# One transformer block (HGRN2, convolution, SwiGLU): the low part of the channel mixer's operand moves from GpSimd to VectorE

## What is computed

```python
x = x + mx[2] * rms_norm(mix_x, post_mix_g[l])
hx = swiglu(modulate(x, pre_ffn_g[l], mx[3], mx[4]), ffn_w_gate[l], ffn_w_up[l], ffn_w_down[l])
x = x + mx[5] * rms_norm(hx, post_ffn_g[l])
# swiglu(h, wg, wu, wd) = (silu(h @ wg) * (h @ wu)) @ wd,  modulate(x, g, shift, scale) = rms_norm(x, g) * (1 + scale) + shift
```

## Time and profile before

| what | value |
|---|---|
| median of 3 runs | 1452.11 us (1450.2 to 1452.63) |
| the profiled execution | 1452.88 us, span 1451.1 us, mean granted PE clock 0.97 |
| PE busy | 1375.9 us (95%) |
| DVE busy | 778.6 us (54%) |
| ACT busy | 377.3 us (26%) |
| GpSimd busy | 324.2 us (22%) |
| `mix(0)` on PE starts | 662.50 us |
| the first `gate_up` starts | 704.28 us |
| the first `gate_up` of the third position starts | 734.13 us |

### The profile page before, as it was taken

One profiled execution on the slowest core, in us unless ns is written; L12 is line 12 of the kernel. 1 busy time (PEld: TensorE's weight loads), 2 busy tenths in 40 slices (PEclk: granted clock), 3 DMA queues, 4 the chain that ended last, 5 costly groups with the idle time before them and its releaser, 6 DMA issues. The chain is left out here.

```text
span 1451.1 us, 17647 instructions
## 1 busy us (share of the span) xinstructions
PE 1375.9 (95%) x6725; PEld 1148.5 (79%) x6725; DVE 778.6 (54%) x1020; ACT 377.3 (26%) x562; POOL 324.2 (22%) x135
## 2 busy tenths in 40 slices
PE   6699899999999997898989999999999999999998
PEld 1588788888888886687768888888888888888876
DVE  2899969769778879818721313232232313232227
ACT  3521222132232234616631121111111121111112
POOL 1522111021111124503524122122122122122110
PEclk9699799999999998999999999999999999999999
DMA  9384110110010010004321111101101111101132
GB/s 370 155 284 165 29 30 16 30 44 28 29 43 29 14 68 34 1 25 164 136 68 29 50 39 58 58 31 57 57 29 58 49 39 57 58 30 57 51 124 116
DMA packets 94704, 101.94 MB, mean 70 GB/s; under 512 B 3118, under 2 KB 77091, under 8 KB 94658
## 3 DMA queue, kind: packets, MB, share of 16 engines
q1 hardware_dynamic: 94658, 101.32, 20.5%
HBM read 92.92 MB, written 8.39 MB: 70 GB/s over the span
## 5 line engine op out<-in xcount | busy, mean ns | idle before, releaser
L1238 POOL TENSOR_TENSOR slot<-slotraw,slot 128x1024 fp32r<-128x1024 f32 x66 | 160.5, 2442 | 522.2 <-ACT slot L1174 313.8
L561 PE MATMUL bank<-h2Ta,slot 128*128 128x512 f32 x1056 | 247.5, 394 | 5.2 <-POOL slot L1238 4.9
L561 PE MATMUL bank<-slot,mid 128*128 128x512 f32 x1056 | 242.9, 391 | 1.8 <-POOL slot L1238 1.8
L561 PEld LDWEIGHTS bank<-h2Ta,slot 128*128 128x128 f32 x1056 | 200.4, 190 | 47.8 <-POOL slot L1238 5.3
L561 PEld LDWEIGHTS bank<-slot,mid 128*128 128x128 f32 x1056 | 199.3, 189 | 43.8 <-POOL slot L1238 2.2
L561 PE MATMUL bank<-cathi,slot 128*128 128x512 f32 x704 | 220.2, 389 | 0.0
L1419 DVE SCALAR_TENSOR_TENSOR cat<-conv_u,taps,cat 128x784 f32 (+29 forms) x120 | 150.6, 1255 | 12.6 <-DVE cat L1419 6.2
L561 PEld LDWEIGHTS bank<-cathi,slot 128*128 128x128 f32 x704 | 132.1, 188 | 27.7 <-issue 0.3
L561 PE MATMUL bank<-hT,ringb 128*128 128x512 f32 (+1 forms) x672 | 149.1, 378 | 0.4 <-DVE cat L1402 0.4
L1694 DVE TENSOR_TENSOR mid<-bank,sgm 128x512 f32<-128x512 f32 x44 | 30.4, 692 | 221.7 <-ACT sgm L1189 221.7
L1719 DVE TENSOR_TENSOR arena<-bank,arena 128x512 f32<-128x512 f32 x144 | 99.5, 691 | 90.0 <-PE bank L561 89.5
(11 more groups left out here) (171 smaller groups left out, 1516.7 us busy)
## 6 DMA issues: line engine op xcount, KB each, us to landing
mraw<-in_w_mod SPq DMA_DIRECT2D x48, 512.0 KB, 7.0
slotraw<-in_ffn_w_gate SPq DMA_DIRECT2D x22, 512.0 KB, 3.7
slotraw<-in_ffn_w_up SPq DMA_DIRECT2D x22, 512.0 KB, 3.8
slotraw<-in_ffn_w_down SPq DMA_DIRECT2D x22, 512.0 KB, 3.9
ringinb<-in_w_in SPq DMA_DIRECT2D x12, 512.0 KB, 3.6
xst<-in_x SPq DMA_DIRECT2D x8, 512.0 KB, 13.7
ringina<-in_w_in SPq DMA_DIRECT2D x8, 512.0 KB, 4.7
ringinc<-in_w_in SPq DMA_DIRECT2D x8, 512.0 KB, 4.7
```

The costliest lines, as they stand in the source:

```text
L561: return pe.matmul(o, l, r, start=start, stop=stop, skip_group_check=True)
L1238: return pool.tensor_tensor(lo, full, hi.bitcast(F32), ALU.subtract)
```

## The change

DVE makes the low part of h2: in step t it does so for block t - 1, behind `x2(t)`, and it waits for ACT's copy (`h2_hi`) there. GpSimd keeps the splits of the four weight slots and nothing else in this stage.

```diff
--- before.py
+++ after.py
@@ -1278,11 +1278,8 @@
                 pool.wait_ge(f_hi, no + 1)
                 lo_part(slot[i][:, 1], slot_raw[i][:, 1], slot[i][:, 0]).then_inc(f_lo, 1)
 
-            for t in range(XT):
-                pool.wait_ge(h2_hi, t + 1)
-                lo_part(h2_block(t, 1), h2f[:], h2_block(t, 0)).then_inc(h2_lo, 1)
-                if t in (0, 1, 3, 5):
-                    ffn_lo((t + 1) // 2, (t + 1) // 2)
+            for j in range(4):
+                ffn_lo(j, j)
 
             def pool_round(n, par):
                 if not first(n):
@@ -1671,6 +1668,11 @@
                                             gain2[:, k:k + 1], mod[:, 3, k, 0:1], ALU.mult, ALU.add)
                 ins.then_inc(h2_free, 1)
 
+            def h2_low(t):
+
+                dve.wait_ge(h2_hi, t + 1)
+                dve.tensor_tensor(h2_block(t, 1), h2f[:], h2_block(t, 0).bitcast(F32), ALU.subtract).then_inc(h2_lo, 1)
+
             mix_add(0)
             for t in range(XT + 1):
                 if t < XT:
@@ -1681,6 +1683,8 @@
                     h2(t - 1)
                 if t < XT:
                     x2(t)
+                if t >= 1:
+                    h2_low(t - 1)
 
             def dve_pair(n, pair, par):
 
```

## The result

The changed kernel takes **1461.15 us** (median of 4 runs, 1460.44 to 1462.54), the kernel before 1451.87 us (4 runs): a ratio of 1.0067, 95% interval 1.0049 to 1.0084, or 9.3 us more. It is slower, as forecast, and 3.3 us less so than the 1464.5 said, within the stated range of 1457 to 1468 us.

A forecast was written before the change was run, and what follows sets the result against it. PE, busy 95% of 1451.1 us, bounds the kernel with its stops. Head, loop and collisions give 10.8 us, clock 1.25: 12.0 on 1452.88 is 1464.9, stated as 1464.5 after half the profile's offset; range 1457 to 1468.

The forecast's parts named there:

- Term 1: Head of the stage: GpSimd's early weight splits hold the SBUF port against DVE, so PE resumes 2.2 us late.
- Term 2: DVE's loop: the low part waits for ACT's copy with x1 behind it, 8.1 us a block against PE's 7.7.
- Term 3: Two more port collisions: GpSimd's splits of slots 2 and 3 make x1(4) and x1(6) 2.0 us late each.
- Rival A: DVE and GpSimd share SBUF rather than exclude, or GpSimd's first splits come later: about +5, 1458 us; chance 0.12.
- The sum at the third position: At the gate_up that started at 734.13: 10.8 us late at turn2(7) plus 1.25 us of clock, 12.0 us.
- What follows moves along one for one: Behind the gate_up that started at 734.13: all later work shifts by the same 12.0 us, nothing added or regained.
- The range: Whole kernel: 9 to 15 us slower, chance 0.75; stated as 1457 to 1468 us.
- Rival B: In DVE's loop, ACT's copy is already made if ACT's chain is at least 2 us shorter: 1452 us; chance 0.05.

The follow-up runs named there:

- run 4: Kernel before with only GpSimd's list changed, splits of slots 0 and 1 ahead of all low parts: 1450.68 us, ratio 0.9993.
- run 3: Changed kernel with DVE's low part one step later in its list, right behind the next x1: 1451.23 us, ratio 0.9998 to the kernel before.
- run 7: Changed kernel with each low part made twice in a row on DVE: 1467.98 us (one run).
- run 1: Changed kernel without GpSimd's four splits of the first round's weights, the high part multiplied instead: 1453.3 us, ratio 1.0013 to the kernel before.
- run 5: Kernel before, unchanged, profiled a second time: the gate_up of the third position came 71.61 us after the start of mix(0), against 71.63.
- run 8: Changed kernel with the low part behind the next x1 and GpSimd's first two splits held back behind x1(1): 1447.5 us, ratio 0.9971 to the kernel before.
- run 10: Kernel before with two fills on DVE ahead of x2(7), as a pure delay: median 2.5 us above the kernel before.

## Why the prediction was right, and where it was off

- **Term 1, the head, 2.2 us**: measured 2.25 (11.03 less 8.78). Shown by the rows of the changed kernel and by run 4, which has the early splits alone.
- **Term 2, the loop of 8.1 us**: measured 8.11. That the wait for ACT's copy makes it, not DVE's work, is shown by run 3 (7.12 a block with the same work), and that it bounds the stage by run 7.
- **Term 3, two collisions of 2.0 us**: x1(4) and x1(6) took 3.22 for 1.28, 1.9 each. Run 1 takes them out. Both end 1.1 us after GpSimd's split does (697.88 + 2.48 = 700.36 and 701.45; 726.04 and 727.12), as the rows of the prediction do: the operation waits, and the two do not merely slow each other. Rival A (1458 us) needed the opposite. Run 1 shows what the kernel takes without any collision, 1453.3; A's price was too high: its walk had `turn2(7)` 4.7 us late, where run 1 has 2.9, with no clock lost behind the stop ahead of the first gate_up.
- **The sum at the third position, 12.0 us late**: measured 12.25 and 11.75. Two sizes were off and nearly cancel: the clock behind the first stop cost 2.3 and 1.6 us in the two profiles for 1.65, which brought `turn2(7)` 11.3 and 10.5 us late for 10.8, and behind the second 2.6 and 2.8 for 2.9. That both lie near the working is in part luck, since they change from one execution to the next. One reading was wrong without a price here: I took the 1.64 us of clock of the kernel before as what set its third position, and looked at `low(7)` in the changed kernel only. `low(7)` held it there as well (run 5), which is why runs 3 and 8, where neither is in the way, came out better than I expected.
- **"What follows moves along one for one"** is the step that failed. The instructions do, and the stops keep their 4.89 and 1.81 us, but the clock behind them costs 2.8 us less (2.3 less in the second pair of profiles). 12.25 - 2.8 = 9.5 and 11.75 - 2.3 = 9.5; measured from the start of `mix(0)` to the end are 9.3 in both pairs. So the term that was mis-sized is the clock of the late stops, taken as +0, measured -2.8. At the delay of run 10, 2.9 us, the late stretches cost what they cost before, and there the step holds. (The idle ahead of the last stop starts at 1402.4 us, not at 1399.)
- **The range.** 9.3 us lies inside the 9 to 15 only just, and not by what set the 9: that bound stood for a cheap clock behind the two stops of the stage, which cost 2.3 and 2.6. The late stops were in no bound. So that the time fell within 9 to 15 is partly luck; the stated 1457 to 1468 holds it with 4 us to spare.
- **Rival B** (no slower, 1452 us) is what run 3 measured, but not by the condition that it named, an ACT chain 2 us shorter. There DVE finds the copy already made because its low part stands one step later in the list. The Trainium skill (GPSIMD Engine Reference, section 4.1) gives elementwise work to VectorE, GpSimd being about twice as slow for two inputs. The durations here agree (1.23 us for a low part, 2.39 on GpSimd), but they do not settle the time: the same operations on the same engines cost 9.3 us in the change and nothing in run 3, and in run 8, with the splits held back, 4.5 us were gained.

## What to carry to other kernels

An operation that is moved to a faster engine takes over that engine's list. Ask what it waits for there and what stands behind it: here 1.2 us of work, placed between a wait for ACT and the instruction at which ACT's next work starts, made a loop of DVE and ACT (8.11 us) longer than PE's time for a block (7.7), and one step later in the list it cost nothing. When it leaves the slow engine's list, look at what moves up in that list, and at which operations of the other engine have to wait for it then: here two splits came forward into the head and cost 2.25 us.

## What the runs showed of the hardware that I had not expected

What PE loses to the lower clock (1.2 GHz) behind a stop is not fixed by the stop. Behind 2.6 us of idle it lost 1.6 us in one profile of a kernel and nothing in the next. Behind 1.81 us it lost 1.6 us or nothing, the same in both profiles of each of three kernels and in kernels with nearly the same delay of the stage, and a delay of all that followed by 1.9 us switched it. A difference of 1 to 3 us between two kernels with such stops can be this alone: run 4 has a stage 2.1 us longer and a median 0.9 us lower. Of the 4.5 us that run 8 gains, 1.3 are the stage and most of the rest (2.8 by the profiles) lies there; another edit ahead of the late stops can take it back.

Two things stay open. What in the program's timing the clock's falls are tied to was not tried. And single executions of one kernel still spread over 3 us; up to 2.2 us of that lie ahead of `mix(0)` in the profiles, and no run looked for their cause.
